# Windowed attention: scores taken two pairs ahead, one masked copy per unit, four probability buffers, values ahead of the transposes

## The chip, the cores and the metric

The kernel runs on 1 core of one Trainium2 chip. The metric is the device time of one execution in microseconds. A kernel is run several times and the median counts.

## The reference, cut to what matters

A two-layer transformer backbone over 512 latent tokens of width 1024 with a prefix of 256 context tokens. Layer 0 mixes tokens with windowed attention (8 query heads in 2 groups, head width 64) beside a Fourier transform; layer 1 uses a gated MLP; each layer ends with an expert FFN that fetches rows of large tables. All of it is float32. Each layer is modulated by vectors that come from `silu(cond) @ ada_w`, 12 matrices of 1024 x 1024 in all. The part that matters here is the attention of layer 0:

```python
# q blocks of 128 tokens; keys: the block before, its own and the next, and 256 context keys
mask = (abs(qi - kj) <= 128) & (kpos >= 0) & (kpos < S)
s_loc = where(mask, q @ k_near.T * scale, -1e30)
s_ctx = q @ k_ctx.T * scale
m = max(s_loc.max(), s_ctx.max(), sink)
den = exp(s_loc - m).sum() + exp(s_ctx - m).sum() + exp(sink - m)
o = (exp(s_loc - m) / den) @ v_near + (exp(s_ctx - m) / den) @ v_ctx
```

## The kernel before, in words

The program is a row of stages, and each stage ends with a barrier of all engines: the front (norms, modulation vectors 0 and 1, projections, rotation), attention, Fourier mixing, and then for each layer a mixing and expert stage, where tables are streamed through TensorE and rows are gathered by GpSimd. Attention is `attention_phase` (L519); it runs from 115.6 us to 247.3 us of the profiled execution.

**Units and pairs.** The work is cut into 32 units `u`: 4 blocks `n` of 128 queries, 4 heads `j` in a group, 2 groups `g`, with `g` fastest. Two units with the same `n` and `j` are a pair (16 pairs, 8 units per block). A unit has 2 near key blocks at the edges (n = 0 and 3) and 3 in the middle, beside 256 context keys, so its row is 512 or 640 wide.

**What each engine does for a unit.** Each engine has a queue of its own, in the order in which the program was written, and the engines wait for each other by semaphores.
- TensorE (PE): `scores(pair)` (L567) multiplies queries with keys into two PSUM tiles `ps_s`, one per group, near keys in one half and context keys in the other. There is one such tile per group, so the scores of a pair can start only when the copies of the pair before are made (semaphores `sc` and `ctx`). `turn(u)` (L581) transposes the probabilities in 4 or 5 blocks into `ps_t`, of which there is one; it waits for the division (`norm`) and for the copy of the unit before out of `ps_t` (`pt`). `values(n)` (L594) multiplies a block's turned probabilities with the values into `ps_o`.
- VectorE (DVE): `front(u)` (L686) copies the near scores out of PSUM block by block, with the mask added at the sides (L698, L700), takes the row maximum (L707) and makes the negative bias in two small instructions (L710, L713). `back(u)` (L715) adds the sums (L721), inverts (L723) and multiplies the probabilities (L725). The order is front(u+1), back(u).
- ScalarE (ACT): `context(u)` (L639) copies the context scores (L644), `exponentials(u)` (L646) computes the exponentials with their sum (L654) and the sink's (L656), `evacuate` (L618) copies turned probabilities out of `ps_t` (L627), `high_half` (L631) copies `ps_o`. The order is context(u+1), exponentials(u), evacuate(u-1).
- `s_sb` (scores in SBUF), `prob` and `stat` have two buffers each, taken in turn by `u % 2`.

**The modulation vectors.** Ten further matrices of `ada_w` are multiplied during attention, as 20 half matrices ("steps") of 512 columns and 2 MB each. `Modulations.multiply(pe, step)` (L184) puts 8 matmuls in the PE queue at the units of the table `STEP_AT`; step 20 (`COLUMNS`) turns the result into columns (L177) at unit 31. Before steps 10 and 20 ScalarE copies the bank (`keep`, L197). There is room for four half matrices. SP issues the load of step s, 4 transfers of 512 KB (L163), when the multiply of step s-4 is done (L554 to L556); steps 0 to 3 are loaded in the front stage. Ahead of these loads SP issues the mask, the sinks and the Fourier tables (2 MB and 128 KB).

```python
STEP_AT = {1 + 29 * step // 20: step for step in range(mods.HALVES)}   # L538
...
scores(0)                                                               # L606
for u in range(len(units)):
    if u % 2 == 0 and u + 2 < len(units):
        scores(u // 2 + 1)
    turn(u)
    if u >= PER_N and u % PER_N == 0:
        values(u // PER_N - 1)
    if u in STEP_AT:
        mods.multiply(pe, STEP_AT[u])
```

## Time and profile before

| what | value |
|---|---|
| runs | 2818.76, 2812.31 and 2819.08 us, median 2818.76 us |
| profiled execution | 2808.57 us, of which the span of the profile is 2806.8 us |
| busy over the whole span | PE 94%, DVE 72%, ACT 37%, POOL 54% |
| attention stage | 131.7 us of the span (115.6 to 247.3 us) |
| busy in the attention stage | PE 107.2 us, DVE 80.7 us, ACT 65.6 us, POOL 0 |
| mean granted clock of TensorE | 0.98 over the span, 0.91 in the attention stage |

The busy shares of the whole span are an average over stages with different limits. The change touches one stage, which is 4.7% of the span, so the rows to look at are those of that stage. The profiled execution is 10.2 us below the median of the three runs.

### The profile page before, as it was taken

How to read it: one execution, taken by the hardware profiler on the slowest of the kernel's cores; microseconds unless marked ns; L12 is line 12 of the kernel's file. 1: busy time of each engine (PE TensorE's matmuls, PEld its weight loads, DVE VectorE, ACT ScalarE, POOL GpSimd, SP SyncE). 2: the span in 40 equal slices, each digit the busy share in tenths (PEclk: the TensorE clock that was granted, in tenths of full speed). 3: DMA queues.
4: the chain of work that ended last, by engine and by line, in shares of the span. 5: the costliest groups of instructions: out<-in, count | busy, mean ns of one | idle time of the engine just before them, and what ended most of it. 6: DMA issues, size and time to landing. Idle time of an engine off the chain costs nothing. (4 is left out here: it accounts for less than half of the span.)

```text
span 2806.8 us, 37266 instructions
## 1 busy us (share of the span) xinstructions
PE 2632.2 (94%) x13090; PEld 2189.7 (78%) x13090; DVE 2016.2 (72%) x4288; ACT 1046.2 (37%) x2983; POOL 1516.4 (54%) x1133
## 2 busy tenths in 40 slices
PE   6888999999999999999988999999999999999996
PEld 4634688888888878878777978888888887878884
DVE  5463389988778756667678658998877775666667
ACT  3352332388888400000014442258878830000002
POOL 1000353656667745657667654356667674656664
PEclk9998999999999999999999999999999999999998
DMA  8391335999999999999995343799999999999997
GB/s 340 120 386 54 121 135 209 393 365 349 393 409 409 409 404 409 409 409 409 409 362 193 128 152 136 264 388 366 360 394 409 409 408 404 409 409 409 409 409 290
DMA packets 268778, 929.58 MB, mean 331 GB/s; under 512 B 28176, under 2 KB 36400, under 8 KB 266544
## 3 DMA queue, kind: packets, MB, share of 16 engines
q0 software_dynamic: 147456, 536.94, 48.7%
q1 hardware_dynamic: 116976, 386.07, 36.2%
q10 hardware_dynamic: 4160, 4.19, 0.4%
q8 instruction: 104, 1.70, 0.2%
q14 instruction: 82, 0.67, 0.1%
HBM read 920.80 MB, written 6.29 MB: 330 GB/s over the span
## 5 line engine op out<-in xcount | busy, mean ns | idle before, releaser
L1375 PE MATMUL exp_down<-peer_gates,all_ring 128*128 128x256 f32 x2720 | 614.9, 383 | 29.9 <-DMA all_ring<-in_peer_v 28.6
L1348 PE MATMUL exp_out<-peer_both,all_ring 128*128 128x256 f32 x2752 | 618.1, 381 | 8.8 <-DMA all_ring<-in_uT 6.4
L1375 PEld LDWEIGHTS exp_down<-peer_gates,all_ring 128*128 128x128 f32 x2720 | 509.1, 190 | 125.2 <-DMA all_ring<-in_peer_v 58.0
L1348 PEld LDWEIGHTS exp_out<-peer_both,all_ring 128*128 128x128 f32 x2752 | 517.0, 191 | 81.0 <-DMA all_ring<-in_uT 12.2
L1193 POOL DMA_INDIRECT all_xT<-in_u_rows,peer_eidx x278 | 355.2, 1278 | 163.6 <-DVE peer_dots L1974 103.3
L1981 DVE SCALAR_TENSOR_TENSOR peer_both<-all_xT,peer_dots,peer_both 128x1024 f32<-128x1024 f32 x226 | 298.0, 1319 | 150.7 <-DMA all_xT<-in_peer_v,peer_eidx 140.7
L1193 POOL DMA_INDIRECT all_xT<-in_peer_v,peer_eidx x230 | 284.8, 1238 | 185.7 <-DVE peer_both L1981 150.7
L1974 DVE CUSTOM_DVE_ANT_0 all_xT<-all_xT,peer_both 128x1024 f32<-128x1024 f32 x278 | 338.5, 1223 | 63.3 <-DMA all_xT<-in_u_rows,peer_eidx 60.9
L1375 PE MATMUL exp_down<-peer_gates,spare_ring 128*128 128x256 f32 x1376 | 316.8, 384 | 12.9 <-DMA spare_ring<-in_peer_v 12.9
L1593 ACT ACTIVATE spare_heavy<-all_iota_b,spare_index 128x128 f32<-128x128 bf16 x1024 | 314.2, 410 | 0.0
L1348 PE MATMUL exp_out<-peer_both,spare_ring 128*128 128x256 f32 x1344 | 304.8, 380 | 5.4 <-DMA spare_ring<-in_uT 4.3
L1981 DVE SCALAR_TENSOR_TENSOR peer_both<-late,peer_dots,peer_both 128x1024 f32<-128x1024 f32 x168 | 228.0, 1357 | 112.4 <-DMA late<-in_peer_v,peer_eidx 106.4
L1375 PEld LDWEIGHTS exp_down<-peer_gates,spare_ring 128*128 128x128 f32 x1376 | 258.5, 191 | 61.4 <-DMA spare_ring<-in_peer_v 26.1
L1348 PEld LDWEIGHTS exp_out<-peer_both,spare_ring 128*128 128x128 f32 x1344 | 251.2, 190 | 39.6 <-DMA spare_ring<-in_uT 6.8
L1193 POOL DMA_INDIRECT late<-in_peer_v,peer_eidx x168 | 201.7, 1200 | 121.7 <-DVE peer_both L1981 96.9
L1597 ACT ACTIVATE spare_heavy<-spare_heavy,spare_share 128x128 f32<-128x128 f32 x512 | 212.0, 502 | 0.0
L1166 POOL TENSOR_TENSOR ask_w_lo<-ask_third,ask_w_hi 128x1024 fp32r<-128x1024 f32 x14 | 33.6, 2403 | 276.1 <-ACT ask_w_hi L1513 276.1
L1641 ACT ACTIVATE ending_gated<-exp_down,all_ada 128x256 f32<-128x256 f32 x8 | 3.0, 489 | 472.6 <-PE exp_down L1375 472.6
L1193 POOL DMA_INDIRECT peer_gates<-in_u_rows,peer_eidx x94 | 117.0, 1244 | 94.4 <-DVE peer_dots L1974 58.4
L1365 PEld LDWEIGHTS exp_down<-spare_heavy 128*128 128x128 f32 x1024 | 132.3, 192 | 26.8 <-ACT spare_heavy L1601 11.3
L1681 ACT ACTIVATE bridge_w_hi<-bridge_raw 128x1024 fp32r<-128x1024 f32 x37 | 38.9, 1052 | 295.7 <-DMA bridge_raw<-in_w_gs_in 292.1
L1365 PE MATMUL exp_down<-spare_heavy 128*128 128x128 f32 x1024 | 137.6, 278 | 11.7 <-issue 5.5
(346 smaller groups left out, 4203.4 us busy)
## 6 DMA issues: line engine op xcount, KB each, us to landing
all_ring<-in_uT SPq DMA_DIRECT2D x172, 512.0 KB
all_ring<-in_peer_v SPq DMA_DIRECT2D x170, 512.0 KB
spare_ring<-in_peer_v SPq DMA_DIRECT2D x86, 512.0 KB
spare_ring<-in_uT SPq DMA_DIRECT2D x84, 512.0 KB
mix_raw<-in_ada_tiles SPq DMA_DIRECT2D x80, 512.0 KB, 9.6
bridge_raw<-in_w_gs_in SPq DMA_DIRECT2D x32, 512.0 KB
all_ring<-in_w_peer_q SPq DMA_DIRECT2D x20, 512.0 KB, 3.6
mix_raw<-in_ada_tiles SPq DMA_DIRECT2D x8, 1024.0 KB, 17.7
```

The source lines that it names most:

```text
L1166: nc.gpsimd.tensor_tensor(q.w_lo[m % 3][:, :, :], asked[m % 3][:, :, :], f32(q.w_hi[m % 3][:, :, :]), ALU.subtract).then_inc(s_lo, 1)
L1193: nc.gpsimd.indirect_dma_start(out=rows[j], out_offset=None, in_=t["u_rows"] if n < HALF else t["peer_v"], in_offset=bass.IndirectOffsetOn ...
L1348: mm = nc.tensor.matmul(outs[:, c % 2, 0:DENSE], raw[c % R][:, k, :], hd[:, k, :], start=(k == 0), stop=(k == KD - 1))
L1365: mm = nc.tensor.matmul(ps_g[g % 2][:, half * TG // 2 + k, :], heavy[:, 1, k, :], heavy[:, 0, k, :], start=True, stop=True)
L1375: mm = nc.tensor.matmul(dn[:, m, :], raw[at % R][:, m, :], gates[:, :, c, :], start=(c == 0 and m % 2 == 0), stop=(c == NKEYS - 1), skip_g ...
L1593: act.activation(heavy[:, side, k, :], iota[:, :, 0], ACT.Abs, scale=2.0, bias=q.index[:, b, side, first + k:first + k + 1]).then_inc(s_ap ...
L1597: act.activation(heavy[:, 0, k, :], heavy[:, 0, k, :], ACT.Relu, bias=q.share[:, b, 0, first + k:first + k + 1], scale=q.share[:, b, 1, fi ...
L1641: act.activation(ending.gated[:, m, :], dn[:, m, :], ACT.Copy, scale=gate[:, m:m + 1]).then_inc(s_egate, 1)
L1681: act.activation(bridge.w_hi[bridge.set_of(i)][:, :, :], bridge.raw[i % 3][:, :, :], ACT.Copy).then_inc(s_bhi, 1)
L1974: nc.vector.tensor_tensor_reduce(out=row, in0=row, in1=own[:, b, :], scale=1.0, scalar=0.0, op0=ALU.mult, op1=ALU.add, accum_out=q.dots[:, ...
L1981: nc.vector.scalar_tensor_tensor(out=acc[:, b, :], in0=row, scalar=q.dots[:, b, k:k + 1], in1=acc[:, b, :], op0=ALU.mult, op1=ALU.add).the ...
```

## The change

It has six parts.
- PE takes scores two pairs ahead: scores(0), step 0, scores(1), and then scores(pair + 2) in front of the turns of a pair. `values(n)` stands in front of turn(8n + 8) instead of behind it.
- `STEP_AT`: step 0 goes behind scores(0). Steps 1 to 19 stand at units 1, 2, 4, 5, 7, 8, 10, 11, 13, 14, 16, 17, 19, 20, 22, 23, 25, 26, 28 (before, steps 0 to 19 stood at 1, 2, 3, 5, 6, 8, 9, 11, 12, 14, 15, 16, 18, 19, 21, 22, 24, 25, 27, 28).
- DVE does front for both units of the next pair, then back for both of this one. ACT does exponentials for two units, context for the next two, and then the evacuations of the pair before.
- `prob` and `stat` have four buffers, so an exponential waits for the turn of u-4. `s_sb`, `ps_s`, `ps_t` and `ps_o` stay as they were.
- The mask gets a middle part of zeros; `front` adds it in one instruction over all near keys. The mask is loaded in two transfers.
- The bias is made in one instruction, min(-scale * max, -sink), with `floor` = -sink made once.

```diff
--- before.py
+++ after.py
@@ -519,23 +519,25 @@
 def attention_phase(nc, t, qkT, kcT, vT, vcT, ident, hi, lo, tables, mods):
 
     with Room(nc, "attn") as r:
-        mask = r.sb("mask", [P, 2, P])
+        mask = r.sb("mask", [P, 3, P])
         sink = r.sb("sink", [P, HEADS])
+        floor = r.sb("floor", [P, HEADS])
         v = r.sb("v", [P, NB + NCB, P])
         s_sb = [r.sb(f"scores{j}", [P, KEYS]) for j in range(2)]
-        prob = [r.sb(f"prob{j}", [P, KEYS]) for j in range(2)]
+        prob = [r.sb(f"prob{j}", [P, KEYS]) for j in range(4)]
         pT = [r.sb(f"probT{j}", [P, KEYS // P, Q_PER_KV, P]) for j in range(2)]
-        stat = r.sb("stat", [P, 2, 8])
+        stat = r.sb("stat", [P, 4, 8])
         ps_s = [r.ps(f"ps_s{j}", [P, 2, 512]) for j in range(2)]
         ps_t = r.ps("ps_t", [P, 2, 512])
         ps_o = r.ps("ps_o", [P, 512])
-        names = ("in", "vt", "v", "s", "sc", "ctx", "mx", "nm", "exp", "den", "rec", "norm", "tr", "pt", "pv",
+        names = ("in", "vt", "v", "floor", "s", "sc", "ctx", "mx", "nm", "exp", "den", "rec", "norm", "tr", "pt", "pv",
                  "ohi", "olo", "dft")
         q = {x: r.sem(x) for x in names}
         block = r.block()
         units = [(n, g, j) for n in range(NB) for j in range(Q_PER_KV) for g in range(KV_HEADS)]
         PER_N = KV_HEADS * Q_PER_KV
-        STEP_AT = {1 + 29 * step // 20: step for step in range(mods.HALVES)}
+        PAIRS = len(units) // 2
+        STEP_AT = {1 + 3 * (step - 1) // 2: step for step in range(1, mods.HALVES)}
         STEP_AT[len(units) - 1] = mods.COLUMNS
 
         def spans(n):
@@ -544,7 +546,8 @@
 
         @block.sync
         def _(sp):
-            sp.dma_start(mask[:, :, :], t["band_mask"]).then_inc(q["in"], 16)
+            for side in range(2):
+                sp.dma_start(mask[:, 2 * side, :], t["band_mask"][:, side, :]).then_inc(q["in"], 16)
             sp.dma_start(sink[:, :], t["attn_sink"].partition_broadcast(P)).then_inc(q["in"], 16)
 
             chan, seq_c, seq_s = tables
@@ -588,7 +591,7 @@
                 blocks = len(spans(n)) + NCB
                 for b in range(blocks):
                     mm = nc.tensor.transpose(ps_t[:, b // 4, (b % 4) * P:(b % 4 + 1) * P],
-                                             prob[u % 2][:, b * P:(b + 1) * P], ident[:, :])
+                                             prob[u % 4][:, b * P:(b + 1) * P], ident[:, :])
                 mm.then_inc(q["tr"], 1)
 
             def values(n):
@@ -604,13 +607,14 @@
                 mm.then_inc(q["pv"], 1)
 
             scores(0)
+            mods.multiply(pe, 0)
+            scores(1)
             for u in range(len(units)):
-                if u % 2 == 0 and u + 2 < len(units):
-                    scores(u // 2 + 1)
+                if u % 2 == 0 and u // 2 + 2 < PAIRS:
+                    scores(u // 2 + 2)
+                if u >= PER_N and u % PER_N == 0:
+                    values(u // PER_N - 1)
                 turn(u)
-                if u >= PER_N and u % PER_N == 0:
-
-                    values(u // PER_N - 1)
                 if u in STEP_AT:
                     mods.multiply(pe, STEP_AT[u])
             values(NB - 1)
@@ -647,26 +651,33 @@
                 n, g, j = units[u]
                 c = len(spans(n)) * P
                 act.wait_ge(q["nm"], u + 1)
-                if u >= 2:
-                    act.wait_ge(q["tr"], u - 1)
-                st = stat[:, u % 2, :]
+                if u >= 4:
+                    act.wait_ge(q["tr"], u - 3)
+                st = stat[:, u % 4, :]
                 h = g * Q_PER_KV + j
-                act.activation(prob[u % 2][:, 0:c + CTX], s_sb[u % 2][:, 0:c + CTX], ACT.Exp, bias=st[:, 1:2],
+                act.activation(prob[u % 4][:, 0:c + CTX], s_sb[u % 2][:, 0:c + CTX], ACT.Exp, bias=st[:, 1:2],
                                scale=SCALE, accum_out=st[:, 2:3]).then_inc(q["exp"], 1)
                 act.activation(st[:, 3:4], sink[:, h:h + 1], ACT.Exp, bias=st[:, 1:2]).then_inc(q["exp"], 1)
 
+            def turned(pair):
+                for u in (2 * pair, 2 * pair + 1):
+                    evacuate(act, u)
+                    if u in STEP_AT:
+                        mods.keep(act, STEP_AT[u])
+                if pair >= PER_N // 2 and pair % (PER_N // 2) == 0:
+                    high_half(act, 2 * pair // PER_N - 1)
+
             context(0)
-            for u in range(len(units)):
-                if u + 1 < len(units):
-                    context(u + 1)
-                exponentials(u)
-                if u >= 1:
-                    evacuate(act, u - 1)
-                if u > PER_N and u % PER_N == 1:
-                    high_half(act, u // PER_N - 1)
-                if u - 1 in STEP_AT:
-                    mods.keep(act, STEP_AT[u - 1])
-            evacuate(act, len(units) - 1)
+            context(1)
+            for pair in range(PAIRS):
+                exponentials(2 * pair)
+                exponentials(2 * pair + 1)
+                if pair + 1 < PAIRS:
+                    context(2 * pair + 2)
+                    context(2 * pair + 3)
+                if pair >= 1:
+                    turned(pair - 1)
+            turned(PAIRS - 1)
             high_half(act, NB - 1)
 
         @block.vector
@@ -674,8 +685,10 @@
             dve.wait_ge(q["vt"], 1)
             nc.vector.tensor_copy(v[:, 0:4, :], ps_t[:, 0, :].rearrange("p (b n) -> p b n", n=P))
             nc.vector.tensor_copy(v[:, 4:6, :], ps_t[:, 1, 0:2 * P].rearrange("p (b n) -> p b n", n=P)).then_inc(q["v"], 1)
-            dve.wait_ge(q["in"], 32)
-            done = [0]
+            nc.vector.memset(mask[:, 1, :], 0.0).then_inc(q["floor"], 1)
+            dve.wait_ge(q["in"], 48)
+            nc.vector.tensor_scalar(floor[:, :], sink[:, :], -1.0, None, ALU.mult).then_inc(q["floor"], 1)
+            dve.wait_ge(q["floor"], 2)
 
             def low_half(n):
                 dve.wait_ge(q["ohi"], n + 1)
@@ -686,52 +699,47 @@
             def front(u):
 
                 n, g, j = units[u]
-                st = stat[:, u % 2, :]
-                c = len(spans(n)) * P
+                st = stat[:, u % 4, :]
+                near = spans(n)
+                c = len(near) * P
                 h = g * Q_PER_KV + j
                 dve.wait_ge(q["s"], u + 1)
                 if u >= 2:
                     dve.wait_ge(q["exp"], 2 * (u - 1))
-                for i, (b, side) in enumerate(spans(n)):
-                    part = slice(i * P, (i + 1) * P)
-                    if side is None:
-                        last = nc.vector.tensor_copy(s_sb[u % 2][:, part], ps_s[u % 2][:, 0, part])
-                    else:
-                        last = nc.vector.tensor_tensor(s_sb[u % 2][:, part], ps_s[u % 2][:, 0, part], mask[:, side, :],
-                                                       ALU.add)
-                    last.then_inc(q["mx"], 1)
-                    done[0] += 1
-                dve.wait_ge(q["mx"], done[0])
-                dve.sem_inc(q["sc"], 1)
+                m = near[0][0] - n + 1
+                nc.vector.tensor_tensor(s_sb[u % 2][:, 0:c], ps_s[u % 2][:, 0, 0:c],
+                                        mask[:, m:m + len(near), :].rearrange("p b n -> p (b n)"),
+                                        ALU.add).then_inc(q["sc"], 1)
+                dve.wait_ge(q["sc"], u + 1)
                 dve.wait_ge(q["ctx"], u + 1)
                 nc.vector.reduce_max(st[:, 0:1], s_sb[u % 2][:, 0:c + CTX], AX.X).then_inc(q["mx"], 1)
-                done[0] += 1
-                dve.wait_ge(q["mx"], done[0])
-                nc.vector.tensor_scalar(st[:, 4:5], st[:, 0:1], SCALE, sink[:, h:h + 1], ALU.mult, ALU.max).then_inc(q["mx"], 1)
-                done[0] += 1
-                dve.wait_ge(q["mx"], done[0])
-                nc.vector.tensor_scalar(st[:, 1:2], st[:, 4:5], -1.0, None, ALU.mult).then_inc(q["nm"], 1)
+                dve.wait_ge(q["mx"], u + 1)
+                nc.vector.tensor_scalar(st[:, 1:2], st[:, 0:1], -SCALE, floor[:, h:h + 1], ALU.mult,
+                                        ALU.min).then_inc(q["nm"], 1)
 
             def back(u):
 
                 n, g, j = units[u]
-                st = stat[:, u % 2, :]
+                st = stat[:, u % 4, :]
                 c = len(spans(n)) * P
                 dve.wait_ge(q["exp"], 2 * (u + 1))
                 nc.vector.tensor_tensor(st[:, 5:6], st[:, 2:3], st[:, 3:4], ALU.add).then_inc(q["den"], 1)
                 dve.wait_ge(q["den"], u + 1)
                 nc.vector.reciprocal(st[:, 6:7], st[:, 5:6]).then_inc(q["rec"], 1)
                 dve.wait_ge(q["rec"], u + 1)
-                nc.vector.tensor_scalar(prob[u % 2][:, 0:c + CTX], prob[u % 2][:, 0:c + CTX], st[:, 6:7], None,
+                nc.vector.tensor_scalar(prob[u % 4][:, 0:c + CTX], prob[u % 4][:, 0:c + CTX], st[:, 6:7], None,
                                         ALU.mult).then_inc(q["norm"], 1)
 
             front(0)
-            for u in range(len(units)):
-                if u + 1 < len(units):
-                    front(u + 1)
-                back(u)
-                if u >= PER_N and u % PER_N == 2:
-                    low_half(u // PER_N - 1)
+            front(1)
+            for pair in range(PAIRS):
+                if pair + 1 < PAIRS:
+                    front(2 * pair + 2)
+                    front(2 * pair + 3)
+                back(2 * pair)
+                back(2 * pair + 1)
+                if pair > PER_N // 2 and pair % (PER_N // 2) == 1:
+                    low_half(2 * pair // PER_N - 1)
             low_half(NB - 1)
             mods.take_rest(dve)
 
```

## Rows read from the trace of the kernel before

**Rows 1.** Page, traffic in 40 slices of 70.2 us of the span.
```profile
GB/s 340 120 386 54 121 135 209 393 365 349 393 409 409 409 404 409 409 409 409 409 362 193 128 152 136 264 388 366 360 394 409 409 408 404 409 409 409 409 409 290
```
**Rows 2.** Stretches: busy time by engine in us (instructions), granted clock, DMA share, GB/s.
```profile
130.00:135.00 5.00, 4.81 (x43) 1.78 (x36) 3.78 (x14) 2.71 (x9) 0.00 (x0) 1.00 0.96 338
...
185.00:190.00 5.00, 5.00 (x42) 2.16 (x34) 3.70 (x11) 4.49 (x14) 0.00 (x0) 1.00 1.05 387
...
215.00:220.00 5.00, 5.00 (x44) 2.02 (x36) 2.85 (x9) 2.55 (x8) 0.00 (x0) 1.00 0.52 192
...
115.60:247.30 131.70, 107.17 (x686) 46.01 (x686) 80.73 (x280) 65.63 (x183) 0.00 (x0) 0.91 0.75 274
```
**Rows 3.** Waits, 115 to 247.3 us: engine, line, releaser, us, times, longest.
```profile
PE attn_ps_t L590 <- DVE attn_prob L725: 17.5, 15, 2.3
```
**Rows 4.** Transfers, 115 to 247 us: issues, KB each, median us to landing.
```profile
mix_raw<-in_ada_tiles SPq DMA_DIRECT2D x64, 512.0 KB, 9.5
```
**Rows 5.** Timeline, SP, 128 us: start, length, engine, line, names.
```profile
128.17 1.89 SPq L163 DMA_DIRECT2D mix_raw<-in_ada_tiles  x3
```
**Rows 6.** Timeline, start of the stage, PE and DVE; idle before and releaser in brackets.
```profile
118.62 0.29 DVE L698 COPY attn_scores<-attn_ps_s 128x128 f32<-128x128 f32 x1 [1.04 <-DMA attn_sink<-in_attn_sink]
...
120.89 1.22 PE L575 MATMUL attn_ps_s<-mix_mixT 64*128 64x256 f32 x4 [3.30 <-DVEq L705]
```
**Rows 7.** Timeline, PE, block 0 of queries.
```profile
128.04 0.70 PE L575 MATMUL attn_ps_s<-mix_mixT 64*128 64x256 f32 x4
...
129.10 0.66 PE L590 MATMUL attn_ps_t<-all_ident,attn_prob 128*128 128x128 f32 x4
...
129.69 1.92 PE L170 MATMUL mix_bank<-mix_raw,mix_cond 128*32 128x512 f32 x16
```
**Rows 8.** Timeline, PE, block 2 of queries.
```profile
194.18 0.92 PE L575 MATMUL attn_ps_s<-mix_mixT 64*128 64x384 f32 x4
...
195.45 0.77 PE L590 MATMUL attn_ps_t<-all_ident,attn_prob 128*128 128x128 f32 x5
...
198.55 0.78 PE L590 MATMUL attn_ps_t<-all_ident,attn_prob 128*128 128x128 f32 x5 [2.33 <-DVE attn_prob L725]
...
199.26 3.55 PE L170 MATMUL mix_bank<-mix_raw,mix_cond 128*32 128x512 f32 x16
```
**Rows 9.** Timeline, DVE, one unit of block 1.
```profile
157.67 0.29 DVE L700 TENSOR_TENSOR attn_scores<-attn_ps_s,attn_mask 128x128 f32<-128x128 f32 x1 [1.33 <-PE attn_ps_s L578]
...
158.50 0.82 DVE L707 TENSOR_REDUCE attn_stat<-attn_scores 128x1 f32<-128x640 f32 x1
...
159.36 0.21 DVE L710 TENSOR_SCALAR attn_stat<-attn_stat,attn_sink 128x1 f32<-128x1 f32 x1
...
159.61 0.15 DVE L713 TENSOR_SCALAR attn_stat<-attn_stat 128x1 f32<-128x1 f32 x1
...
160.53 0.28 DVE L700 TENSOR_TENSOR attn_scores<-attn_ps_s,attn_mask 128x128 f32<-128x128 f32 x1
```
**Rows 10.** Timeline, PE, end of the stage and first matmuls of the next.
```profile
227.85 1.92 PE L170 MATMUL mix_bank<-mix_raw,mix_cond 128*32 128x512 f32 x16
...
232.71 0.66 PE L590 MATMUL attn_ps_t<-all_ident,attn_prob 128*128 128x128 f32 x4 [2.08 <-DVE attn_prob L725]
...
234.14 1.09 PE L590 MATMUL attn_ps_t<-all_ident,attn_prob 128*128 128x128 f32 x4 [0.78 <-ACT attn_probT L627]
...
235.02 3.44 PE L177 MATMUL mix_bank<-mix_pick,mix_flat 128*128 128x20 f32 x16
...
238.39 6.20 PE L601 MATMUL attn_ps_o<-attn_probT,attn_v 128*64 128x512 f32 x16
...
247.33 2.90 PE L759 MATMUL fft_ps_a<-mix_chan,mix_mixT 128*128 128x256 f32 x6 [2.75 <-PEq L94]
```
**Rows 11.** Lines by shape, 115.6 to 247.3 us: count, busy us, mean ns, idle before.
```profile
L601 PE MATMUL attn_ps_o<-attn_probT,attn_v 128*64 128x512 f32 x72 | 18.9, 675 | 0.0
```
**Rows 12.** Timeline, PE, the front stage: column matmuls at full clock.
```profile
25.11 1.95 PE L177 MATMUL mix_bank<-mix_pick,mix_flat 128*128 128x2 f32 x16 [0.72 <-ACT mix_flat L371]
```

More of the change, by code:

```diff
@@ L606, in _ @@
             scores(0)
+            mods.multiply(pe, 0)
+            scores(1)
             for u in range(len(units)):
-                if u % 2 == 0 and u + 2 < len(units):
-                    scores(u // 2 + 1)
-                turn(u)
+                if u % 2 == 0 and u // 2 + 2 < PAIRS:
+                    scores(u // 2 + 2)
                 if u >= PER_N and u % PER_N == 0:
                     values(u // PER_N - 1)
+                turn(u)
                 if u in STEP_AT:
```

## The prediction

> **What bounds the kernel now.** I read the page's traffic slices first. From the eighth slice on, but for a dip between the layers, the kernel moves 350 to 409 GB/s: the expert tables stream, and that is its long part [rows 1]. The attention stage lies in the second to fourth slice. It ends at a barrier, after which the next stage issues its own loads, so nothing later has started early, and a microsecond saved inside the stage should reach the end of the program whole. So the question is only what bounds these 131.7 us.
>
> I read the stage's own stretch next: PE is busy 107.17 us of 131.70, DVE 80.73, ACT 65.63, at a mean granted clock of 0.91 [rows 2]. PE is nearest to its limit and not at it. It waits 17.5 us at the transposes for the division on DVE [rows 3]. The timeline shows why: with two probability buffers and scores only one pair ahead, the second unit of a pair is divided long after its first (195.45 to 198.55), and the multiply behind that wait takes 3.55 us where another takes 1.92, the clock having fallen to its lower level after 2.33 us of idle PE [rows 7, 8].
>
> The traffic shows a second limit. From about 133 us the loads of the half matrices run without a gap at 387 GB/s; in 215 to 220 us the mean is 192, that is 0.96 MB, which at 387 ends at 217.5 us [rows 2]. Sixteen steps of four 512 KB transfers [rows 4] are 16 x 2.10 MB, and at 387 GB/s a step takes 5.42 us. The multiply of step 19 begins at 227.85 [rows 10]. So the loads have only 10.3 us of slack, and whatever the engines gain beyond that, the loads take back unless they start earlier.
>
> **The change part by part.** I cut the stage at the end of step 1's multiply, which releases the load of step 5, and at the end of step 19's.
>
> *Start to the end of step 1.* Before, this ends at 129.69 + 1.92 = 131.6 us [rows 7]. DVE's first copy starts at 118.62 and is released by the sinks' transfer [rows 6]. After: the second mask transfer puts the sinks one issue later and `floor` adds a small instruction and a wait; neither is in the trace, so I bound them together between 0 and 1.0 us and take 0.7 (L710 to L713, a small dependent pair, takes 0.25 [rows 9]). That gives 119.3. A front of a 640-wide unit takes 2.0 us now (157.67 to 159.61, and the issue of L713); it loses one small instruction, 0.25 [rows 9]. The single masked copy is not in the trace: the maximum starts 0.83 us after the first of three copies (157.67 to 158.50), and a copy of one third of the width lasts 0.29 [rows 9], so the gain lies between 0 and 0.5 and I take 0.15. The narrow unit I put at 1.45. The first transposes now wait for four fronts instead of two, and front(2) waits for scores(1), which start at front(1)'s copy, 121.4, on a PE that has idled since step 0; before, these scores ran cold too, 1.22 us against 0.70 warm [rows 6, 7], about 2.1 us in all. So front(2) starts at 123.5, front(3) ends at 126.4, back(0) takes 0.85, and turn(0) starts at 127.2. Turn to turn with an evacuation between takes 1.43 (232.71 to 234.14 [rows 10]), so turn(1) is at 128.7 to 129.2 and the multiply ends between 131.2 (warm) and 133.7 (cold). I take **132.6**, 1.0 later than before. Step 0's multiply, in front of all this, costs nothing: it fills 1.9 us in which PE waited 3.30 us anyway [rows 6]; without that cover it would cost its 1.92.
>
> *Step 1 to step 19, by loads.* Step 4's load now leaves after step 0, near 120 us, behind the Fourier tables, and lands near 130 us. Step 5's cannot leave before step 1's end, 132.6. Then the queue never runs dry, since each later multiply has about 2 us or more to spare. From first issue to first data took about 2.1 us: the issue was at 128.17 [rows 5], and the 1.69 MB moved in 130 to 135 us [rows 2] need 4.4 us at 387 GB/s. So step 19 has landed at 132.6 + 2.1 + 15 x 5.42 = 216.0 and its multiply ends at **217.9**.
>
> *The same stretch by PE's work.* Thirteen pairs of scores, 5 narrow at 1.06 and 8 wide at 1.27 (128.04 to 129.10, 194.18 to 195.45): 15.5. Twenty-seven turns, 11 at 0.59 and 16 at 0.71 (129.10 to 129.69, 198.55 to 199.26): 17.9. Seventeen multiplies (steps 2 to 18) at 1.9: 32.3 [rows 7, 8]. Three values, 18.9 less the cold last one of 6.2: 12.7 [rows 10, 11]. Sum 78.4. In four pairs (units 6, 12, 18 and 24) no multiply follows the even turn, so the next waits out the evacuation, 1.43 - 0.59 = 0.84 each: 3.4. Total 81.8, against 83.4 by the loads. The two limits nearly coincide; the loads bind narrowly, and for places where they alternate I add **1.0**. Before, this stretch took 227.85 - 131.61 = 96.2.
>
> *What hides the rest.* DVE's cycle for a wide unit is 2.86 (157.67 to 160.53) and becomes about 2.46 [rows 9]: at most 79 us for 32 units in a stage of about 115, so the masked copy and the shorter bias are worth nothing directly. If PE and loads were out of the way, they would be worth 0.4 a unit, 13 us. ACT issues what it did, 65.6 us [rows 2]. Its new order puts the evacuation of unit 2p behind two exponentials and two context copies; I cost that at nothing because these were released a pair earlier, and where a multiply follows the turn PE has 1.9 us of cover. Moving the values only moves PE's work.
>
> *Step 19 to the end.* Now 17.5 us (229.77 to 247.3): the turns wait 2.08 us, and then the columns (3.44) and values (6.20) run at the lower clock [rows 10]. After, with the probabilities waiting in four buffers: three turns 1.43 apart, 0.6 for the last, columns 1.95 as in the front stage [rows 12], values 3.65 (the other three's 12.7 is one narrow and two wide), and 247.33 - 244.59 = 2.7 for what follows: about 11.9 warm. At the lower clock it is 17.2. The rows show the clock falling after idle stretches of 2.1 to 2.3 us, and here the gaps are 0.8, so I take 12.6, near the warm end.
>
> The Trainium skill, page "TensorE: Matmul & The Clock Gate", section "Loop structure matters more than you think", says that a wait for a transfer between matmuls sends the clock down, while a vector copy in between does not. By that rule this tail, which follows a multiply that waits for its load, would start cold: 17.2 instead of 12.6, and a gain smaller by 4.6. The trace bears out only part of it: the slow multiply of 199.26 followed a wait for DVE, so the idle time counts here and not who ended it [rows 8].
>
> **Sum.** 132.6 + 83.4 + 1.9 + 1.0 + 12.6 = 231.5 for the end of the stage, against 247.3: 15.8 us less. Against the profiled execution's own 2808.6 us (span 2806.8 and 1.8 around it) that is 2792.8. This execution was 10.2 us below the median of the runs, so on the median's footing I say 2818.8 - 15.8 = **2803**.
>
> **The rivals.**
> - *ACT's order bites* (gain 0 to 10). Each evacuation stands behind exponentials that wait for DVE. ACT works 65.6 us, 4.1 a pair [rows 2]; if in 13 pairs PE waits another 0.5 to 1.0 us, 6.5 to 13 us are lost: 2812 in the middle. For it: one `ps_t`. Against it: the exponentials are released a pair early. Chance 0.18, about half of it a gain above 8.4 us.
> - *Loads do not bind and the tail is warm* (gain over 20). It needs step 1 to end at 131 and PE's 81.8 to count: 2797. Chance 0.05.
> - *The clock falls and stays* (slower). The late first turn leaves PE nearly idle for some 5 us, and the gaps between transposes keep it at the lower of its two levels, 1.2 GHz. Place: all PE work between step 1 and step 19. Price: 3.55 for 1.92, that is 0.85 us per microsecond of full-speed work [rows 7, 8]. It decides from 15.8 / 0.85 = 18.6 us of such work on; with 40 us of the 78 the kernel takes 2803 + 34 = 2837. Against it: the clock came back each time here, and the gaps get fewer. Chance 0.04.
> - *Nothing comes of it*, as the head start of the pipeline is lost at its slow start and the loads only move: the gain stays within 4 us, 2818. Chance 0.03.
>
> **How the numbers follow.** The forecast (gain 10 to 20) has 0.70. A measurement can tell about 0.3% from no change, 8.4 us. Faster by more: 0.70 + 0.05 + 0.09 = 0.84. Within: 0.09 + 0.03 = 0.12. Slower: 0.04. The range covers the forecast's own (2799 to 2809) with the 6 us by which runs of one kernel differ, and most of the first two rivals: 2793 to 2815.
>
> **What would show it.** Right: step 0 near 117.5 us; traffic near 387 GB/s without a gap from 135 to about 216; step 19's multiply near 216 and waiting for its load, not for DVE; the granted clock 1.00 from 135 on, few waits of PE for the division; the stage ending at 229 to 234; the stages behind it unchanged. Wrong: step 1 ending after 134 (start mis-sized); step 19's multiply after 219 with its load long there (ACT's order, a wait of transposes for L627's evacuation); columns over 3 us (cold tail); the saving in the stage not reaching the span.

## The result and the profile after

The changed kernel takes 2804.6 us (median of 7 runs, 2800.47 to 2806.87) against 2816.44 us before (7 runs). The medians differ by 11.8 us. The ratio of the two kernels is given as 0.9946, with a 95% interval of 0.9927 to 0.9964, which is 10 to 21 us faster, with 15 in the middle. The forecast was 2803 us.

The profiled execution has a span of 2798.7 us, 8.1 us below the one before. The attention stage alone, from SP's first issue to the first Fourier matmul, went from 131.7 us (115.6 to 247.3) to 118.0 (115.16 to 233.15), a gain of 13.7. Behind the stage the changed kernel's profile is 6 us longer, which takes back part of this. Two profiles of the changed kernel itself differ by as much there, as the table in the next section shows, so it is not read as an effect of the change.

Stretches of the changed kernel (columns as in [rows 2]):

```profile
130.00:135.00 5.00, 5.00 (x32) 1.85 (x28) 1.68 (x6) 2.54 (x9) 0.00 (x0) 0.67 0.21 33
...
185.00:190.00 5.00, 4.05 (x34) 1.96 (x32) 3.64 (x10) 4.04 (x14) 0.00 (x0) 1.00 1.05 387
...
200.00:205.00 5.00, 3.24 (x16) 0.60 (x16) 1.34 (x5) 1.91 (x7) 0.00 (x0) 0.66 1.06 386
...
215.00:220.00 5.00, 4.22 (x36) 1.93 (x32) 3.99 (x12) 3.10 (x10) 0.00 (x0) 1.00 0.27 101
...
115.20:233.20 118.00, 101.00 (x687) 43.49 (x687) 73.61 (x202) 65.77 (x183) 0.00 (x0) 0.94 0.84 306
```

PE is busy 101.00 of 118.00 us, where it was busy 107.17 of 131.70, at a clock of 0.94 instead of 0.91 [rows 2]. The work is the same; its busy time is 6.2 us shorter because less of it ran at the lower of the clock's two levels. The traffic stops between 130 and 135 us (33 GB/s), since step 4's load has landed and step 5's is not yet released, and then runs at 387 GB/s until 215 + 0.51 MB / 387 GB/s = 216.3 us.

PE's waits in the stage (engine, operation, releaser: us, times, longest):

```profile
PE attn_ps_t L593 <- ACT attn_probT L631: 7.8, 11, 0.9
...
PE attn_ps_s L578 <- DVE attn_scores L710: 4.3, 2, 2.5
...
PE mix_bank L170 <- DMA mix_raw<-in_ada_tiles: 2.4, 1, 2.4
```

The 17.5 us for the division [rows 3] are gone. What is late now is the evacuation of the single `ps_t`, and once a load. Before, these waits within the stage added up to 21.6 us (17.5 for the division, 3.3 for the first scores and 0.8 for an evacuation); now they are 14.5. So of the 13.7 us about 7 are shorter waits and about 6 are work that ran at the higher clock. Part of the 6 is luck: the columns and last values ran 4.1 us faster than before, and in the changed kernel's second profile, with a stage of 119.3, 1.7 of this was lost again.

Timeline of PE in the changed kernel, answering to [rows 6 to 10]:

```profile
117.05 1.92 PE L170 MATMUL mix_bank<-mix_raw,mix_cond 128*32 128x512 f32 x16
...
124.37 1.23 PE L578 MATMUL attn_ps_s<-mix_mixT 64*128 64x256 f32 x4 [2.50 <-DVE attn_scores L710]
...
126.38 1.11 PE L593 MATMUL attn_ps_t<-all_ident,attn_prob 128*128 128x128 f32 x4
...
129.29 3.64 PE L170 MATMUL mix_bank<-mix_raw,mix_cond 128*32 128x512 f32 x16
...
187.79 0.74 PE L593 MATMUL attn_ps_t<-all_ident,attn_prob 128*128 128x128 f32 x5 [0.94 <-ACT attn_probT L631]
...
198.60 0.74 PE L593 MATMUL attn_ps_t<-all_ident,attn_prob 128*128 128x128 f32 x5 [0.30 <-ACT attn_probT L631]
...
201.76 3.50 PE L170 MATMUL mix_bank<-mix_raw,mix_cond 128*32 128x512 f32 x16 [2.42 <-DMA mix_raw<-in_ada_tiles]
...
220.04 1.92 PE L170 MATMUL mix_bank<-mix_raw,mix_cond 128*32 128x512 f32 x16
...
224.74 0.63 PE L593 MATMUL attn_ps_t<-all_ident,attn_prob 128*128 128x128 f32 x4 [0.78 <-ACT attn_probT L631]
...
225.21 1.86 PE L177 MATMUL mix_bank<-mix_pick,mix_flat 128*128 128x20 f32 x16
...
227.00 3.65 PE L604 MATMUL attn_ps_o<-attn_probT,attn_v 128*64 128x512 f32 x16
...
233.15 3.69 PE L767 MATMUL fft_ps_a<-mix_chan,mix_mixT 128*128 128x256 f32 x16 [2.50 <-PEq L94]
```

Step 0 fills the wait at the start (117.05). The first turn comes at 126.38, step 1's multiply is slow (3.64 us), step 16 at 201.76 waits 2.42 us for its load and is slow behind it, and the columns and values of the end run at full clock (1.86 and 3.65 us against 3.44 and 6.20 [rows 10]).

Three lines of the changed kernel's second profile ("changed again" below): step 1, step 16 and the last values.

```profile
129.72 1.93 PE L170 MATMUL mix_bank<-mix_raw,mix_cond 128*32 128x512 f32 x16
...
201.07 3.64 PE L170 MATMUL mix_bank<-mix_raw,mix_cond 128*32 128x512 f32 x16 [2.80 <-DMA mix_raw<-in_ada_tiles]
...
227.59 5.32 PE L604 MATMUL attn_ps_o<-attn_probT,attn_v 128*64 128x512 f32 x16
```

### The profile page after: what moved, and what is told of

It is laid out like the page before. It is cut to its first block and busy times, and to the rows that moved or that the text cites. A ratio compares the mean times of both kernels' runs of the same rounds, so it can differ in the third digit from the quotient of the medians.

```text
span 2798.7 us, 37187 instructions
## 1 busy us (share of the span) xinstructions
PE 2629.4 (94%) x13090; PEld 2185.8 (78%) x13090; DVE 2012.5 (72%) x4210; ACT 1046.9 (37%) x2983; POOL 1487.6 (53%) x1133
## 5 line engine op out<-in xcount | busy, mean ns | idle before, releaser
L1201 POOL DMA_INDIRECT all_xT<-in_peer_v,peer_eidx x230 | 258.5, 1124 | 198.5 <-DVE peer_both L1989 165.0
L1201 POOL DMA_INDIRECT spare_row<-in_u_rows,peer_eidx x68 | 90.5, 1330 | 111.8 <-DVE peer_dots L1982 66.1
```

Of the source, the lines that this page charges most:

```text
L1201: nc.gpsimd.indirect_dma_start(out=rows[j], out_offset=None, in_=t["u_rows"] if n < HALF else t["peer_v"], in_offset=bass.IndirectOffsetOn ...
```

## The experiments

Each run gives one profile. "Stage" is the time from SP's first issue of attention to the first Fourier matmul; "rest" is from there to the end of the span.

| kernel | from - to | stage us | rest us |
|---|---|---|---|
| before | 115.63 - 247.33 | 131.7 | 2559.5 |
| changed | 115.16 - 233.15 | 118.0 | 2565.5 |
| x1 three copies | 116.54 - 236.69 | 120.2 | 2563.0 |
| x2 values behind | 116.28 - 232.12 | 115.8 | 2563.5 |
| x3 three buffers | 116.11 - 245.52 | 129.4 | 2563.7 |
| x4 step 1 in front | 114.61 - 231.03 | 116.4 | 2569.7 |
| x5 small loads | 116.13 - 230.92 | 114.8 | 2567.7 |
| x6 before, masked copy | 115.18 - 240.10 | 124.9 | 2558.4 |
| x7 before, new steps | 114.68 - 243.91 | 129.2 | 2565.6 |
| x8 one pair ahead | 116.19 - 300.04 | 183.9 | 2559.8 |
| x9 evacuations first | 115.33 - 265.35 | 150.0 | 2565.3 |
| x11 three buffers, evacuations first | 114.67 - 275.10 | 160.4 | 2569.7 |
| changed again | 116.13 - 235.41 | 119.3 | 2559.3 |
| y1 even places | 115.58 - 226.82 | 111.2 | 2563.2 |

The rest lies between 2558 and 2570 us and does not follow the stage's length; in the two profiles of the changed kernel it differs by 6.2 us. That is why the spans of before and changed differ by 8.1 us and their stages by 13.7, and why small effects are read from the stage and not from the whole. The stages of these two profiles differ by 1.3 us, so for a difference of 1 or 2 us between single profiles I look up where in the stage it arises.

**DVE's part undone (x1).**
```diff
-nc.vector.tensor_tensor(s_sb[..][:, 0:c], ps_s[..][:, 0, 0:c], mask[:, m:m + len(near), :], ALU.add)
+for i, (b, side) in enumerate(spans(n)):
+    ...   # one copy or masked copy per key block
-nc.vector.tensor_scalar(st[:, 1:2], st[:, 0:1], -SCALE, floor[:, h:h + 1], ALU.mult, ALU.min)
+nc.vector.tensor_scalar(st[:, 4:5], st[:, 0:1], SCALE, sink[:, h:h + 1], ALU.mult, ALU.max)
+nc.vector.tensor_scalar(st[:, 1:2], st[:, 4:5], -1.0, None, ALU.mult)
```


> The changed kernel with only its DVE part undone: near scores copied block by block again, the bias in two instructions (84 short instructions more). The stage is read from the first SP issue of attention to the first Fourier matmul: 131.7 us before, 118.0 us changed. Theory 1 (the stage is bound by PE's queue and by the chain of loads, DVE has slack): wide units cost DVE 0.4 us more, a pair 5.7 us against about 6.9 us of PE, so the stage takes 118 to 120.5, the 0.8 of the two first fronts among it. Theory 2 (the gain came from the shorter DVE cycle): 32 x 0.4 = 13 us are lost and the stage takes 129 to 131.

```profile
116.50:236.70 120.20, 102.36 (x687) 44.03 (x687) 81.29 (x282) 65.89 (x183) 0.00 (x0) 0.93 0.82 300
```

DVE is busy 81.29 us (the third of the busy times) where it was 73.61, and the stage takes 120.2, 2.2 more. That is Theory 1: DVE has slack in the new order. The clock is no part of the 2.2, as the same two multiplies ran slow (3.64 and 3.57 us) and the last values took 3.65 in both; 1.0 of it arises before the end of step 1.

**The same part alone (x6)**: the reverse of x1's edit, made in the kernel before.

> The kernel before with only the masked copy in one instruction and the short bias (and the mask with its middle part). Order, buffers and steps as before. In that kernel PE waits 17.5 us for the division, so DVE's cycle is in the path: Theory 1 expects 0.25 to 0.4 us from about half of the 32 units, 4 to 8 us: stage 124 to 128. Theory 2 (the gain of the change is DVE's shorter cycle): 13 us, stage 119.

The waits of PE for the division in x6:

```profile
PE attn_ps_t L592 <- DVE attn_prob L721: 12.1, 10, 2.2
```

12.1 us instead of 17.5 [rows 3], and a stage of 124.9, a gain of 6.8: 5.4 in these waits, and 1.5 in PE's busy time (105.68 us against 107.17), which is the clock. In the old order DVE was in PE's path, in the new one hardly: the same edit is worth 6.8 us alone and 2.2 beside the rest. The parts don't add up.

**Values back behind the turn (x2).**
```diff
-if u >= PER_N and u % PER_N == 0: values(u // PER_N - 1)
 turn(u)
+if u >= PER_N and u % PER_N == 0: values(u // PER_N - 1)
```


> The changed kernel with only the values put back behind the turn of unit 8n+8. Theory 1: PE does the same work in another order; the evacuation of that unit waits for 3.7 to 4.5 us of values, while PE is busy with them, so 0 to 3 us are lost in three places: stage 118 to 121. Theory 3 (moving the values is the main gain, since in the kernel before ACT waited 12.3 us for them in three places): stage 126 to 130.

The stage takes 115.8, 2.2 less than the changed kernel and below both expectations. All of it arises before the end of step 1's multiply, which ran at full clock here (1.92 us, against 3.64), as did the transposes just before it; the changed kernel's second profile has the same fast start. Behind step 1 the two stages are equal within 0.2 us: where the values stand is worth nothing.

**Only the new places of the steps (x7)**: the kernel before with step 0 behind scores(0) and the new table.

> The kernel before with only the new places of the steps: step 0 behind scores(0), the others by the new table. Theory 1: step 0's multiply (1.9 us) goes into a wait of PE at the start, and step 1 a unit earlier; the chain of loads has slack in that kernel, so nothing else: stage 129 to 130. Rival (the order of the steps was the main gain, as loads bound the kernel before too): stage 122 or less.

The stage takes 129.2, a gain of 2.5, and no multiply waits for a load. The kernel before was not bound by its loads. The gain looks like step 0's 1.9 us, but it is not shown to be that: PE's waits for the first scores fell from 3.3 to 1.8 us while those for divisions and evacuations grew (18.3 to 19.5), and PE's busy time fell by 2.0 us, which is the clock.

**Three buffers (x3).**
```diff
-prob = [r.sb(f"prob{j}", [P, KEYS]) for j in range(4)]
+prob = [r.sb(f"prob{j}", [P, KEYS]) for j in range(3)]
-if u >= 4: act.wait_ge(q["tr"], u - 3)
+if u >= 3: act.wait_ge(q["tr"], u - 2)
```


> The changed kernel with three probability buffers instead of four; an exponential waits for the turn of u-3. Theory 1: the exponentials of pair p have long to wait before PE asks for them, and three buffers still let both start ahead of the turn before: stage 118 to 120. Rival (the fourth buffer is needed, since the second exponential of a pair now waits for the first turn of the pair before): 0.3 to 0.6 us in each of 15 pairs, stage 122.5 to 127.

129.4 us is above both expectations. All but 2.3 us of the gain is lost with the fourth buffer. PE's waits for evacuations grew from 7.8 to 18.8 us. One such place:

```profile
PE attn_ps_t L593 <- ACT attn_probT L631: 18.8, 16, 2.5
...
170.83 0.53 PEld L593 LDWEIGHTS attn_ps_t<-all_ident,attn_prob 128*128 128x128 f32 x5 [0.33 <-issue]
...
171.69 0.83 ACT L658 ACTIVATE attn_prob<-attn_scores,attn_stat 128x640 f32<-128x640 f32 x1 [2.13 <-PE attn_ps_t L593]
...
172.71 0.63 ACT L648 ACTIVATE attn_scores<-attn_ps_s 128x256 f32<-128x256 f32 x2
...
173.23 0.76 ACT L631 ACTIVATE attn_probT<-attn_ps_t 128x512 f32<-128x512 f32 x2
...
174.14 0.74 PE L593 MATMUL attn_ps_t<-all_ident,attn_prob 128*128 128x128 f32 x5 [2.54 <-ACT attn_probT L631]
```

PE turns unit 2p at 170.83. Only then may ACT start the exponential of 2p+3 (171.69), and behind it in ACT's queue stand the context copies (172.71) and the evacuation of 2p (173.23), for which PE's next turn has waited 2.54 us when it starts at 174.14. The buffer is paid for by what is queued behind the waiting exponential.

**Evacuations in front of the context copies (x9), and with three buffers (x11).**
```diff
+if pair >= 1: turned(pair - 1)
 if pair + 1 < PAIRS: context(2 * pair + 2); context(2 * pair + 3)
-if pair >= 1: turned(pair - 1)
```


> The changed kernel with ACT's evacuations of the pair before in front of the context copies of the next. Theory 1: the waits of PE for evacuations (0.78 to 0.94 each) are the copy's own length, and the context copies come later by two evacuations, which DVE's slack takes: stage 117 to 120. Rival (ACT's order holds PE up): PE waits 3 to 5 us less, stage 113 to 115.

> Three probability buffers (129.4 us, waits of PE for evacuations 18 to 19 us against 7.8) together with the evacuations in front of the context copies. Theory 4 (with three buffers the second exponential of a pair waits for the first turn of the pair before, and the evacuation which the next turn needs stands behind that exponential and two context copies on ACT): taking the two copies, 0.63 us, out from between gives 0.6 us back in 8 to 15 places, stage 120 to 125, waits for evacuations 9 to 13. Rival (the loss comes from the late exponentials themselves, through DVE's divisions): stage 128 to 131.

Of both runs both theories fell, by far: 150.0 and 160.4 us. In x9:

```profile
PE attn_ps_s L578 <- DVE attn_scores L710: 24.1, 14, 3.3
...
163.16 0.77 ACT L631 ACTIVATE attn_probT<-attn_ps_t 128x512 f32<-128x512 f32 x2 [1.78 <-PE attn_ps_t L593]
...
164.29 0.68 ACT L648 ACTIVATE attn_scores<-attn_ps_s 128x256 f32<-128x256 f32 x2
...
164.79 0.82 DVE L715 TENSOR_REDUCE attn_stat<-attn_scores 128x1 f32<-128x640 f32 x1 [6.63 <-ACT attn_scores L648]
...
166.38 0.92 PE L578 MATMUL attn_ps_s<-mix_mixT 64*128 64x384 f32 x4 [3.26 <-DVE attn_scores L710]
```

An evacuation can't start before PE's turn. With the context copies (164.29) behind the evacuation of the pair's second unit (163.16), DVE's maximum has waited 6.63 us when it starts at 164.79, its copy of the next unit comes behind that, and PE's scores wait 3.26 us for this copy (166.38): PE waits for work that waits for PE. So the largest effect hangs on an order that is not in the headline: ACT must copy the context scores ahead of the evacuations. Swapping the two costs 32 us here. The kernel before had its context copy ahead of its evacuation too, so this is a property that the new order had to keep, and not a part of the gain. In x11 the copies were to leave the path of x3's wait; instead both losses came together.

**Scores one pair ahead (x8)**, with x9's order on ACT, without which it would stand still.
```diff
-if u % 2 == 0 and u // 2 + 2 < PAIRS: scores(u // 2 + 2)
+if u % 2 == 0 and u // 2 + 1 < PAIRS: scores(u // 2 + 1)
```


> The changed kernel with scores only one pair ahead on PE (ACT evacuates before it copies the context, since it would wait in a circle otherwise). DVE still does both fronts of the next pair before the divisions of this one. Theory 1 (the second pair of scores in flight is what takes the waits for the division away): after scores PE waits for two fronts and a division, about 4 us, of which a multiply or two and nothing else cover part: 1.5 to 3 us a pair, stage 140 to 165. Rival (the depth is not needed, four buffers and the pairwise order do it): stage 118 to 122.

```profile
PE attn_ps_t L593 <- DVE attn_prob L729: 47.8, 13, 4.3
```

183.9 us, above both expectations. x9 is its right neighbour (150.0), so with DVE doing two fronts before each pair of divisions the second pair in flight is worth 34 us on top of ACT's order, in waits for the division that reach 4.3 us and in multiplies at the lower clock (PE is busy 16 us longer than in x9). What the second pair or the four buffers would be worth with the unit-by-unit order of the kernel before, no run shows.

**Loads cut to an eighth (x5)**; the modulation vectors are then partly made of stale columns.
```diff
-sp.dma_start(self.place(step)[:, j:j + 2, :], self.tiles[v][:, j:j + 2, h * 512:(h + 1) * 512])
+sp.dma_start(self.place(step)[:, j:j + 2, 0:64], self.tiles[v][:, j:j + 2, h * 512:h * 512 + 64])   # steps 4 to 19
```


> The changed kernel with the loads of steps 4 to 19 cut to 64 of 512 columns, so that they move an eighth; the modulation vectors are then made from stale columns and the output is another. It takes the load chain away and leaves everything else. Theory 1: step 16 no longer waits 2.4 us and does not run slow after it (1.6 us): stage 114.0. Rival (PE's queue alone sets the length, the wait is absorbed): 117 to 118. If the engines also ran faster without the traffic, the durations of single instructions would be shorter than 0.82 and 0.83 us for the wide maximum and exponential.

```profile
197.12 0.74 PE L594 MATMUL attn_ps_t<-all_ident,attn_prob 128*128 128x128 f32 x5 [0.30 <-ACT attn_probT L632]
...
197.79 1.92 PE L171 MATMUL mix_bank<-mix_raw,mix_cond 128*32 128x512 f32 x16
...
214.49 1.93 PE L171 MATMUL mix_bank<-mix_raw,mix_cond 128*32 128x512 f32 x16
...
219.66 2.63 PE L178 MATMUL mix_bank<-mix_pick,mix_flat 128*128 128x20 f32 x16
...
222.22 6.19 PE L605 MATMUL attn_ps_o<-attn_probT,attn_v 128*64 128x512 f32 x16
```

No multiply waits. From the start of step 2's multiply to the end of step 19's it takes 83.2 us (133.24 to 216.42), the changed kernel 87.25 (134.71 to 221.96): 4.1 us, which is the wait of 2.42 and the 1.58 that the multiply behind it ran slow. The stage is 114.8, only 3.2 less, since the clock differed elsewhere too: the part before step 2's multiply was 2.4 us shorter (step 1 at full clock), and the columns and last values were 3.3 us longer. The wide maximum and exponential last 820 and 825 ns with and without the traffic, so the traffic did not slow these two.

**Step 1 in front as well (x4).**
```diff
 mods.multiply(pe, 0)
+mods.multiply(pe, 1)
 scores(1)
-STEP_AT = {1 + 3 * (step - 1) // 2: step for step in range(1, mods.HALVES)}
+STEP_AT = {1 + 3 * (step - 1) // 2: step for step in range(2, mods.HALVES)}
```


> The changed kernel with step 1's multiply moved up behind step 0's, in front of scores(1), where PE waits. Its load is long there. Theory 1: it leaves the queue where it took 3.64 us at the lower clock, and the load of step 5 is issued about 10 us earlier, so the 2.4 us wait of step 16 for its load and the 1.6 us that its multiply ran slow go as well: stage 118.0 - 3.6 - 4.0 = 110.4, and no multiply waits for a load. Rival (loads do not bind, step 16's wait was made up for later): only the multiply's place counts, stage 114.4 or more. Rival 2: scores(1) are held up by 1.0 us behind the multiply, and the start is later by that.

```profile
197.91 1.92 PE L170 MATMUL mix_bank<-mix_raw,mix_cond 128*32 128x512 f32 x16 [1.73 <-DMA mix_raw<-in_ada_tiles]
...
219.32 0.63 PE L593 MATMUL attn_ps_t<-all_ident,attn_prob 128*128 128x128 f32 x4 [0.78 <-ACT attn_probT L632]
...
219.78 2.84 PE L177 MATMUL mix_bank<-mix_pick,mix_flat 128*128 128x20 f32 x16
...
222.56 5.97 PE L604 MATMUL attn_ps_o<-attn_probT,attn_v 128*64 128x512 f32 x16
...
231.03 5.20 PE L768 MATMUL fft_ps_a<-mix_chan,mix_mixT 128*128 128x256 f32 x16 [2.51 <-PEq L94]
```

116.4, and step 16 still waited 1.73 us. Step 5's load did leave early, but step 6's waits for step 2, so the chain came forward by at most one load (5.4 us), not by ten us; step 16's multiply starts 3.3 us earlier after the stage's start. The end of step 19's multiply lies 101.9 us behind the stage's start, 4.9 earlier than in the changed kernel; the slow tail took 3.3 of it back.

**A version meant to beat both (y1).** Step 1 goes to the front as in x4, and a multiply behind every even turn is to cover the evacuation that the odd turn waits for. The changed kernel was run again beside it, on the same chip.
```diff
 mods.multiply(pe, 0)
+mods.multiply(pe, 1)
 scores(1)
-STEP_AT = {1 + 3 * (step - 1) // 2: step for step in range(1, mods.HALVES)}
+at = sorted([*range(0, len(units), 2), 7, 23])
+STEP_AT = {u: step + 2 for step, u in enumerate(at)}
```


> A version meant to be better than both: steps 0 and 1 in front of scores(1), and steps 2 to 19 at the units 0, 2, 4, 6, 7, 8, 10, 12, 14, 16, 18, 20, 22, 23, 24, 26, 28, 30, so that a multiply follows every even turn and covers its evacuation; the rest as in the changed kernel. Theory 1: the waits of PE for evacuations (7.8 us in 11 places) shrink to about 1, loads run without a gap from 119 us and the last lands about 96 to 98 us after the stage's start, step 19's multiply ends at 100, and behind it stand one turn, the columns, the last values and 2.7 us: stage 109 to 111 us against 118.0, device time 7 to 9 us below the changed kernel. Rival (the evacuations were no loss, since loads or the other engines take their place): 114 to 117, 1 to 4 us below. Rival 2 (multiplies that wait for their loads let the clock fall): single multiplies of 3.5 us, stage 112 to 116.

> The changed kernel itself again, as the neighbour of the version above on the same chip: 0.9946 of the kernel before, within 0.9927 to 0.9964; stage 116 to 121 us, by whether step 1's multiply and the tail run at full clock (1.7 and 3.3 us).

```profile
PE attn_ps_t L594 <- DVE attn_prob L732: 4.0, 6, 1.6
...
PE attn_ps_t L594 <- ACT attn_probT L633: 2.9, 4, 0.8
...
127.84 3.43 PE L170 MATMUL mix_bank<-mix_raw,mix_cond 128*32 128x512 f32 x16
...
216.14 1.92 PE L170 MATMUL mix_bank<-mix_raw,mix_cond 128*32 128x512 f32 x16
...
218.78 1.96 PE L177 MATMUL mix_bank<-mix_pick,mix_flat 128*128 128x20 f32 x16
...
220.67 3.65 PE L605 MATMUL attn_ps_o<-attn_probT,attn_v 128*64 128x512 f32 x16
...
226.82 5.21 PE L769 MATMUL fft_ps_a<-mix_chan,mix_mixT 128*128 128x256 f32 x16 [2.50 <-PEq L94]
```

Median 2791.56 us (6 runs), ratio to before 0.9918 (0.9893 to 0.9944); the changed kernel on the same chip 2803.16 us (9 runs), 0.9952 (0.9932 to 0.9971). The two intervals overlap, but five of y1's six runs lie below all nine of the changed kernel (2789.64 to 2793.82 against 2796.36 to 2809.82; the sixth took 2802.06), so y1 is very likely the faster. The stages agree: 111.2 us, just above the 109 to 111 expected, against 118.0 and 119.3. Step 2's multiply ran at the lower clock here (3.43 us), else it would have been 1.5 less. The waits for evacuations fell from 7.8 to 2.9 us, not to 1, and no multiply waits for a load; in their place PE waits 4.0 us for divisions, so DVE is back in its path.

Most of the gain is step 1's place and not the even turns. x4, which has only that, would take 113.1 us with a tail at full clock as in y1 (116.4 - 3.3), an estimate from the two tails; the even places add the 1.9 us down to 111.2.

## Why the prediction was right

- *The place and the mechanism.* Shown: with two pairs of scores in flight, four buffers and the order by pairs, the waits for the division (17.5 us) are gone. x3 takes one buffer away, x9 swaps ACT's order and x8 takes the second pair away from x9: they lose 11, 32 and 34 us, and in x8 the waits for the division are back (47.8 us).
- *The number.* 2803 against 2804.6 is closer than the working deserves. It started from a median before of 2818.8, which seven runs put at 2816.4, and took off 15.8 where the medians differ by 11.8.
- *Start.* Step 1's end was put at 132.6 and came at 132.9. That is luck, as two errors cancelled: turn(0) was 0.8 us earlier than worked out (0.5 of it since the whole stage began earlier), and the multiply fully slow.
- *Loads.* The last landing was put at 216.0; the traffic ends at 216.3. But the multiply that met the loads was step 16, not 19. Step 19's came at 220.04 with its load long there, where the prediction had it near 216 and waiting; it had named just this as a sign of being wrong. The term "1.0 for places where the two limits alternate" was mis-sized: it measures 4.0 (x5). I had the bounds meet at the end of the stretch only, whereas PE meets the loads at unit 23, and behind it has its own work still to do, so the wait adds to PE's work instead of standing for it. The likely reason is that PE runs ahead in the pairs that have no values between them. Also, by the prediction's own chain step 16 could start at 132.9 + 2.1 + 12 x 5.42 = 200.1; it started at 201.76, and in the second profile, x1 and x2 it was 1.7 to 2.3 us late as well. Why, is open.
- *PE's work.* Put at 81.8 us for the stretch; x5, without loads, shows 82.8 (131.66 to 214.49). Evacuation waits were put at 3.4 and are 5.5 in eight places. Four are those expected; a fifth stands at unit 28, in front of which there are neither scores nor a multiply, and three stand behind a multiply (0.79, 0.16 and 0.30 us).
- *Tail.* Put at 12.6, it took 11.2, at full clock. The other runs show that this was not sure: x4, x5 and the changed kernel's second profile had part or all of it slow.
- *Costed at nothing.* The masked copy and the bias: 2.2 us in place, so nearly right. Per wide unit the copy saves 0.25 us and the bias 0.20 (from first copy to maximum 0.83 us in x1 and 0.58 in the changed kernel), where the prediction had 0.15 and 0.25. Values: nothing, right. ACT's order: the three waits behind a multiply are its price, 1.3 us. What the prediction did not see is how much would be lost with the other order of copies and evacuations (x9).
- *Sum.* End of the stage 231.5 forecast, 233.2 measured, which is 15.8 and 14.2 us earlier than before; as the stage also began 0.5 earlier, it is 13.7 us shorter. The start was 0.3 too early in the forecast, the stretch to step 19's end 2.7 too short and the tail 1.4 too long.
- *The rule on the clock.* The Trainium skill, page "TensorE: Matmul & The Clock Gate", section "Loop structure matters more than you think", says that a long wait for a transfer before every matmul makes PE go cold. The multiply behind the 2.42 us wait was slow (3.50), as before one behind 2.33 us for DVE [rows 8]; behind 1.73 us in x4 it was not (1.92). So the trace agrees for the longer of these waits, and a wait for DVE did the same. The tail, for which the prediction drew on the rule, came behind a multiply that did not wait for its load, so this case did not arise.

## What to carry to other kernels

In a pipeline over several in-order engines, ask of each queue what stands behind its waiting instruction: one buffer less cost 11 us here, and one swapped pair of lines on an engine that is half idle 32, while 7.7 us of work put back on DVE cost 2.2. An edit's worth alone (x6, 6.8 us) is not its worth beside the others (x1, 2.2). And when loads and compute nearly coincide, lay both out step by step, since the wait can come in the middle, and then the work behind it still has to be done.

## What I had not expected of the hardware

TensorE's clock level differs between executions with the same instructions and nearly the same gaps. After three gaps of 0.78 us, the last values took 3.65 us in the changed kernel, 5.32 in its second profile and 5.97 and 6.19 in x4 and x5; step 1's multiply took 3.64 us in the first profile of the changed kernel and 1.93 in its second. The Fourier stage then begins with 16 matmuls in 3.69 us (changed) or 5.20 (x4). That is up to 1.7 us at step 1, up to 3.3 at the tail and 1.5 behind the stage; what decides it, no run here shows.
